# Expert gate/up with stationary weights and 88 token places, low parts made by two engines, three orders in the sparse layers

## The reference, cut to what matters

```python
def swiglu(h, wg, wu, wd):
    return (jax.nn.silu(h @ wg) * (h @ wu)) @ wd

def moe_swiglu(h, w_router, wg, wu, wd):
    logits = (h @ w_router).astype(jnp.float32)
    top_v, top_i = lax.top_k(logits, TOP_K)            # TOP_K = 2 of N_EXPERTS = 8
    w_top = jax.nn.softmax(top_v, axis=-1)
    gate = jnp.sum(jax.nn.one_hot(top_i, N_EXPERTS, dtype=jnp.float32) * w_top[..., None], axis=-2)
    out = jnp.zeros_like(h)
    for e in range(N_EXPERTS):                         # D_FF_EXPERT = 1408
        out = out + gate[..., e:e + 1].astype(h.dtype) * swiglu(h, wg[e], wu[e], wd[e])
    return out
```

## Time and profile before

| what | value |
|---|---|
| median of 3 runs | 1364.44 us (1361.74 to 1364.74) |
| the profiled execution | 1365.28 us, span 1363.5 us |
| mean granted TensorE clock | 0.993 of 2.4 GHz |
| PE busy / weight loads / DVE / ACT / POOL | 1332.1 / 1170.4 / 963.7 / 766.0 / 111.6 us |
| HBM read | 307.21 MB |

### The profile page before, as it was taken

The page is one execution under the profiler, slowest core; times in us unless marked ns, Lnnn a source line. Parts: engine busy times, 40 slices in busy tenths (PEclk is TensorE's granted clock), DMA queues, the critical chain, the costliest instruction groups (busy, mean ns, idle before and its releaser), DMA issues.

```text
span 1363.5 us, 21446 instructions
## 1 busy us (share of the span) xinstructions
PE 1332.1 (98%) x8477; PEld 1170.4 (86%) x8477; DVE 963.7 (71%) x1355; ACT 766.0 (56%) x927; POOL 111.6 (8%) x126
## 2 busy tenths in 40 slices
PE   7999999999999999999999999999999999999996
PEld 7999889888977898889999889888888888888885
DVE  6466477564867577866544465876988898998897
ACT  5565489334334348734433335753777777777674
POOL 1000031100001210000422010002000000000000
PEclk9999999999999999999999999999999999999998
DMA  7653344446534545425555536434898998999996
GB/s 284 228 191 124 139 143 152 154 159 227 202 126 152 201 176 203 171 108 186 216 186 186 186 132 228 174 126 193 318 362 332 404 361 336 394 330 365 391 421 268
DMA packets 46518, 314.72 MB, mean 231 GB/s; under 512 B 5136, under 2 KB 5392, under 8 KB 10720
## 3 DMA queue, kind: packets, MB, share of 16 engines
q1 hardware_dynamic: 42192, 297.27, 58.0%
q0 software_dynamic: 4240, 16.25, 3.4%
HBM read 307.21 MB, written 6.29 MB: 230 GB/s over the span
## 4 chain that ended last, share of the span: by engine, by line
PE 84%; DVE 7%; DMA 4%; ACT 3%; issue 1%; POOL 0%; SPq 0%; DVEq 0%; ACTq 0%
PE g_ps L647 17%; PE g_ps L649 17%; PE g_ps L648 17%; PE a_ps L647 7%; PE a_ps L649 7%; PE a_ps L648 7%; PE a_ps L652 4%; DMA raw<-w_dram 4%; DVE w_lo L1748 3%; PE a_ps L656 3%; PE o_ps L652 3%; ACT w_hi L1349 1%; DMA arena<-xT_dram 0%; PE g_ps L652 0%; PE g_ps L666 0%
## 5 line engine op out<-in xcount | busy, mean ns | idle before, releaser
L1748 DVE TENSOR_TENSOR w_lo<-raw,w_hi 128x2048 fp32r<-128x2048 f32 x218 | 502.4, 2306 | 178.2 <-ACT w_hi L1349 177.2
L1349 ACT ACTIVATE w_hi<-raw 128x2048 fp32r<-128x2048 f32 x218 | 417.4, 1914 | 251.0 <-PE a_ps L649 118.9
L647 PE MATMUL g_ps<-x_hi,w_hi 128*128 128x256 f32 x848 | 244.2, 288 | 4.7 <-ACT arena L1567 4.5
L648 PE MATMUL g_ps<-x_lo,w_hi 128*128 128x256 f32 x848 | 241.6, 285 | 0.0
L649 PE MATMUL g_ps<-x_hi,w_lo 128*128 128x256 f32 x848 | 241.4, 285 | 0.0
L647 PE MATMUL g_ps<-w_hi,x_hi 128*128 128x512 f32 (+1 forms) x584 | 217.5, 373 | 1.8 <-DVE x_lo L1841 1.0
L649 PE MATMUL g_ps<-w_hi,x_lo 128*128 128x512 f32 (+1 forms) x584 | 212.7, 364 | 0.0
L648 PE MATMUL g_ps<-w_lo,x_hi 128*128 128x512 f32 (+1 forms) x584 | 212.2, 363 | 0.0
L647 PEld LDWEIGHTS g_ps<-x_hi,w_hi 128*128 128x128 f32 x848 | 164.4, 194 | 7.6 <-issue 7.1
L649 PEld LDWEIGHTS g_ps<-x_hi,w_lo 128*128 128x128 f32 x848 | 164.4, 194 | 0.0
L648 PEld LDWEIGHTS g_ps<-x_lo,w_hi 128*128 128x128 f32 x848 | 164.3, 194 | 0.0
(11 more groups left out here) (345 smaller groups left out, 2011.6 us busy)
## 6 DMA issues: line engine op xcount, KB each, us to landing
raw<-w_dram SPq DMA_DIRECT2D x257, 1024.0 KB, 5.7
raw_in_arena<-w_dram SPq DMA_DIRECT2D x21, 1024.0 KB, 7.5
raw<-w_dram SPq DMA_DIRECT2D x4, 512.0 KB, 8.0
arena<-rows_dram POOLq DMA_DIRECT2D x2, 1024.0 KB, 6.0
table_dram<-arena POOLq DMA_DIRECT2D x2, 1024.0 KB, 9.0
arena<-table_dram POOLq DMA_DIRECT2D x2, 1024.0 KB, 13.3
arena<-xT_dram SPq DMA_DIRECT2D x2, 512.0 KB, 5.4
x<-x_dram SPq DMA_DIRECT2D x2, 512.0 KB, 7.5
```

Of the source, the lines that this page charges most:

```text
L647: pe.matmul(ps, lh, rh, start=start, stop=False, skip_group_check=True)
L648: pe.matmul(ps, lh, rl, start=False, stop=False, skip_group_check=True)
L1349: act.activation(w_hi[w_place(s)][:, :], raw[PLACE[s]][:, :], ACT.Copy).then_inc(hi_done, 1)
L1748: dve.tensor_tensor(w_lo[w_place(s)][:, :], raw[PLACE[s]][:, :], w_hi[w_place(s)][:, :].bitcast(F32), ALU.subtract).then_inc(lo_done, 1)
```

## The change

- **88 token places.** CAP = 88 replaces 128 per expert, CHUNKS = 3 rounds at most instead of 2; more than one round only if an expert has over 88 tokens. `sel`, `row_of`, `gate_of`, `back`, `o_hi`, `o_lo`, `o_rows` and `ym` shrink to 88. `x_both` holds, per block of the contraction and per expert, 88 high and 88 low columns side by side.
- **Gate/up.** The weights are the stationary side: per slot two 128-column halves (gate, up) by eight blocks, and for each a matmul of `w_hi` with 176 moving columns and one of `w_lo` with 88. The result comes out as hidden rows by tokens, so the transposes go. DVE sums the two 88-column parts (`joined`, a reduce out of PSUM), ACT applies silu in SBUF, DVE multiplies (`opened`), ACT and DVE split into `ym`. A bank of PSUM now holds one slot instead of a unit.
- **Low parts shared.** From slot MOE + 3 on DVE makes columns 0 to 1279 of `w_lo` and POOL columns 1280 to 2047 (`share`). PE and SP wait for both. POOL's row sends and table reads stand between its shares.
- **Sparse layers.** ACT's `ahead(I_KC)` stands behind the copy of the turned q. `compressed` runs between the two halves of the rows slot of step 7. The two halves of the first output slot run at steps 9 and 10.

```diff
@@ -44,6 +44,9 @@
...
 MOE = 143
+CAP = 88
+CHUNKS = -(-S // CAP)
+SHARED = 1280
 N_SLOTS = MOE + PAIRS * 33
@@ -314,15 +319,15 @@
...
-    return part[:, u % 4 // 2, (u % 2) * S:(u % 2 + 1) * S].rearrange("p (m c) -> p m c", m=2)
-def gate_of_unit(u):
-    return gate_view(u)[:, 0:S].rearrange("p (m c) -> p m c", m=2)
-def unit_half(u, which):
-    return g_ps[u % 3][:, :].rearrange("p (m g c) -> p m g c", m=2, g=2)[:, :, which, :]
+    return part[:, u % 4 // 2, (u % 2) * S:(u % 2) * S + 2 * CAP].rearrange("p (m c) -> p m c", m=2)
+def sums_of(u):
+    return gate_view(u)[:, 0:4 * CAP].rearrange("p (m g c) -> p m g c", m=2, g=2)
+def unit_bank(u, half):
+    return g_ps[(2 * u + half) % 3][:, 0:4 * CAP].rearrange("p (g a c) -> p g c a", g=2, a=2)
@@ -475,6 +481,9 @@
...
+if LAST_THERE[to] >= MOE:
+    sp.sem_inc(half_free, 1)
+    sp.wait_ge(lo_shared, LAST_THERE[to] - MOE + 1 + turn)
@@ -612,23 +621,52 @@
...
+def whole(n):
+    pool.wait_ge(lo_done, MOE + n)
+    pool.sem_inc(lo_shared, 1)
+def share(s, i):
+    slot = s + RING
+    pool.wait_ge(hi_done, slot + 1 + 33 * i)
+    pool.tensor_tensor(w_lo[w_place(slot)][:, SHARED:], raw[PLACE[slot]][:, SHARED:],
+                       w_hi[w_place(slot)][:, SHARED:].bitcast(F32), ALU.subtract).then_inc(lo_shared, 1)
+def send(e, i):
+    pool.wait_ge(m_ohi, 2 * e + 2 + 4 * i)
+    pool.sem_inc(rows_sent, 1)
+    pool.wait_ge(table_rows, 32 + 16 * e + 32 * i)
+    pool.sem_inc(rows_sent, 1)
+    pool.indirect_dma_start(o_table[:, :], bass.IndirectOffsetOnAxis(row_of[0:CAP, e:e + 1], 0),
+                            o_rows[0:CAP, e, :], None).then_inc(table_rows, 16)
+def gate_up(i, earlier):
+    for n in range(FT):
+        share(MOE + n, i)
+        if n == 2 and earlier:
+            send(1, i - 1)
+whole(1)
...
+whole(2)
+whole(3)
...
+gate_up(0, False)
...
-    for e in range(2):
-        pool.wait_ge(m_ohi, 2 * e + 2 + 4 * i)
-        pool.sem_inc(rows_sent, 1)
-        pool.wait_ge(table_rows, 32 + 16 * e + 32 * i)
-        pool.sem_inc(rows_sent, 1)
-        pool.indirect_dma_start(o_table[:, :], bass.IndirectOffsetOnAxis(row_of[:, e:e + 1], 0),
-                                o_rows[:, e, :], None).then_inc(table_rows, 16)
+    for c in range(UNITS):
+        share(MOE + FT + c, i)
+        if c == 8:
+            send(0, i)
+    gate_up(i + 1, True)
...
-pool.wait_ge(sums_in, 16)
-pool.dma_start(f_acc[:, :, :], choice_rows(1), accum_op=ALU.add).then_inc(sums_in, 16)
+for c in range(UNITS - RING):
+    share(MOE + FT + c, before)
+    if c == 4:
+        pool.wait_ge(sums_in, 16)
+        pool.dma_start(f_acc[:, :, :], choice_rows(1), accum_op=ALU.add).then_inc(sums_in, 16)
@@ -1156,16 +1196,17 @@
...
-if i == STEP_KV:
-    compressed()
...
-        rows_slot(s0 + m)
+        rows_slot(s0 + m, compressed if i == STEP_KV else None)
...
-    out_slot(L_WO[l], OUT_L, 0, (c_lo, 2 * l + 1))
+    pe.wait_ge(lo_done, L_WO[l] + 1)
+    out_mm(L_WO[l], OUT_L, 0, 0, (c_lo, 2 * l + 1))
+if i == STEP_OUT[0] + 1:
+    out_mm(L_WO[l], OUT_L, 0, 1).then_inc(used, 1)
@@ -1218,56 +1259,48 @@
...
+        mm = mm32(bank[:, :], back[0:CAP, e, t * P:(t + 1) * P], src[0:CAP, e, n * 512:(n + 1) * 512],
...
+def split_ready(s, i, whole=False):
+    pe.wait_ge(lo_done, s + 1 + 33 * i)
+    if not whole:
+        pe.wait_ge(lo_shared, s - MOE + 1 + 33 * i)
...
+    if earlier:
+        pe.wait_ge(m_xlo, 4 + 4 * i)
...
+            n = 2 * u + half
+            s, e, bank = MOE + n, n // UNITS, g_ps[n % 3]
+            if n >= 3:
+                pe.wait_ge(m_sum, n - 2 + FT * i)
+            elif earlier:
+                pe.wait_ge(m_sum, FT * i)
+            split_ready(s, i, n < RING and not earlier)
+            hi, lo = weights(s, (KD, S))
+            for which in range(2):
+                to, rows = bank[:, 2 * CAP * which:2 * CAP * (which + 1)], slice(which * P, (which + 1) * P)
...
+                    if n == 0 and which == 0 and not earlier and k % 2 == 0:
+                        pe.wait_ge(m_xlo, k // 2 + 1)
+                    pe.matmul(to, hi[:, k, rows], x_both[:, k, e, :, :].rearrange("p a c -> p (a c)"),
+                              start=k == 0, stop=False, skip_group_check=True)
+                    mm = pe.matmul(to[:, 0:CAP], lo[:, k, rows], x_both[:, k, e, 0, :],
+                                   start=False, stop=k == KD - 1, skip_group_check=True)
+            mm.then_inc(used, 1)
+        if u == TURN_SEL_AFTER:
+            if earlier:
+                pe.wait_ge(m_ohi, 4 * i)
...
+                    mm = mm32(a_ps[1][0:CAP, 2 * e:2 * e + 2], sel[:, t, e, :].bitcast(F32),
@@ -1561,10 +1592,11 @@
...
-for m in (0, I_Q[0], I_KC):
+for m in (0, I_Q[0]):
...
+ahead(s0 + I_KC)
@@ -1679,27 +1711,26 @@
...
+act.wait_ge(m_hid, u + 1 + UNITS * i)
+act.activation(ym_hi[:, 2 * u:2 * u + 2, :], hidden_of(u), ACT.Copy).then_inc(m_yhi, 1)
...
+    if u >= 1:
+        y_high(u - 1, i)
...
+    act.wait_ge(m_sum, 2 * u + 2 + FT * i)
+    act.activation(sums_of(u)[:, :, 0, :], sums_of(u)[:, :, 0, :], ACT.Silu).then_inc(m_silu, 1)
...
+    if c == 1:
+        y_high(UNITS - 1, i)
...
+        act.activation(back[0:CAP, :, :], o_ps[0:CAP, :].rearrange("p (a b) -> p a b", a=2), ACT.Copy)
@@ -1745,7 +1776,8 @@
...
-dve.tensor_tensor(w_lo[w_place(s)][:, :], raw[PLACE[s]][:, :], w_hi[w_place(s)][:, :].bitcast(F32),
+mine = slice(0, SHARED if s >= MOE + RING else SLOT)
+dve.tensor_tensor(w_lo[w_place(s)][:, mine], raw[PLACE[s]][:, mine], w_hi[w_place(s)][:, mine].bitcast(F32),
@@ -2457,37 +2491,44 @@
...
+    dve.tensor_tensor(ym_lo[:, 2 * u:2 * u + 2, :], hidden_of(u),
...
+def joined(u, half, i):
+    dve.wait_ge(used, MOE + 2 * u + half + 1 + 33 * i)
+    dve.tensor_reduce(sums_of(u)[:, half, :, :], unit_bank(u, half), AX.X, ALU.add).then_inc(m_sum, 1)
+def opened(u, i):
+    dve.wait_ge(m_silu, u + 1 + UNITS * i)
+    dve.tensor_tensor(hidden_of(u), sums_of(u)[:, :, 0, :], sums_of(u)[:, :, 1, :], ALU.mult).then_inc(m_hid, 1)
...
+            two = a_ps[1][0:CAP, 0:4].rearrange("p (a b) -> p a b", a=2)
+            dve.tensor_scalar(row_of[0:CAP, :], two[:, :, 1], const[0:CAP, C_PART:C_PART + 1], None, ALU.max)
+            dve.tensor_copy(gate_of[0:CAP, :], two[:, :, 0]).then_inc(m_back, 1)
+        joined(u, 0, i)
+        if u >= 1:
+            opened(u - 1, i)
+        ahead(s, i)
+        joined(u, 1, i)
+        if u >= 1:
+            y_low(u - 1, i)
...
+        if c == 0:
+            opened(UNITS - 1, i)
+        if c == 2:
+            y_low(UNITS - 1, i)
```

More of the change, by code:

```diff
@@ L279, in rounded @@
             return nc.alloc_sbuf_tensor_at(name, [P, *shape], F32R, offset=at)
-        sel = rounded("sel", arena_at + 4 * 6656, (NT, 2, P))
+        sel = rounded("sel", arena_at + 4 * 6656, (NT, 2, CAP))
+        x_both = rounded("x_both", x_at, (KD, 2, 2, CAP))
         back = rounded("back", arena_at + 4 * 7680, (2, S))
@@ L682, in rows_slot @@
                 for m in range(2):
+                    if m and amid:
+                        amid()
                     for k in range(KD):
@@ L1304, in down @@
                             for t in range(NT):
-                                tr = turned(o_ps[:, e * S + t * P:e * S + (t + 1) * P], sel[:, t, e, :].bitcast(F32))
+                                tr = turned(o_ps[0:CAP, e * S + t * P:e * S + (t + 1) * P], sel[:, t, e, :].bitcast(F32))
                         tr.then_inc(m_turn_sel, 1)
@@ L1721, in high_out @@
                                 act.wait_ge(used, MOE + FT + 11 + 33 * i)
[L1722 to L1723 removed]
+                            act.activation((o_hi if last else o_rows)[0:CAP, e, n * 512:(n + 1) * 512], a_ps[2 * e + n][0:CAP, :],
+                                           ACT.Copy, scale=gate_of[0:CAP, e:e + 1]).then_inc(m_ohi, 1)
                     gate_up(0)
@@ L2009, in gate_weights @@
                 on1, on2 = t3(32), t3(48)
-                own(dve.tensor_scalar(ranks[:, 0, :, NE:2 * NE], gate, -1.0 - P, None, ALU.add))
+                for half in range(1, CHUNKS):
+                    own(dve.tensor_scalar(ranks[:, 0, :, half * NE:(half + 1) * NE], gate, -1.0 - CAP * half, None, ALU.add))
                 for t in range(NT):
-                    for half in range(2):
+                    for half in range(CHUNKS):
                         own(dve.tensor_scalar(ranks[:, 2, t, half * NE:(half + 1) * NE], on2[:, t, :],
@@ L2466, in gate_up @@
                         s = MOE + 2 * u
-                        ahead(s, i)
                         if u == TURN_SEL_AFTER + 1:
@@ L2588, in expert_slots @@
         two = gu[:, :, 2 * u:2 * u + 2].transpose(1, 0, 2, 3, 4)
-        halves = [two[:, :, m] for m in range(2)] if u == 5 else [two[:, 4 * h:4 * h + 4] for h in range(2)]
-        up += [h.reshape(1, P, SLOT) for h in halves]
+        up += [two[:, :, m].reshape(1, P, SLOT) for m in range(2)]
     return np.concatenate(up + [wd.reshape(FT // 2, 2, P, D).transpose(0, 2, 1, 3).reshape(FT // 2, P, SLOT)])
```

110 lines of the change are left out of this document (24 added, 86 removed).

## The result

The changed kernel takes 1482.5 us (median of 4 runs, 1476.25 to 1487.87) against 1363.1 for the kernel before beside it: ratio 1.088 (95% interval 1.082 to 1.093), 119 us slower. The forecast was 1440, range 1410 to 1485, 0.94 on slower. The direction held, and the time lies inside the range, 43 us above the forecast. The weight loads and the turn-taking are there, but the turns don't set the pace of gate/up, and the 43 us are a term that stood at nothing, TensorE's clock.

A forecast was written before the change was run, and what follows sets the result against it. PE was taken as the bound, its time being columns streamed. Gate/up +65, down +9 and +4, hand-overs +4 gave +82; orders -6: 1365.3 + 82 - 6 = 1441, against the median 1440; range 1410 to 1485.

The forecast's parts named there:

- Loads, 0.111 us each, slot 3.55: Gate/up on PE: 32 weight loads per slot at 0.111 us make 3.55 us, against 2.76 before; +15.0 us per pair.
- rival (a): Expert stage: turns hide, only weight loads count, +60, down unchanged, orders -6: 1419 us; chance 0.18.
- Turn-taking: Expert stage: DVE and POOL alternate on low parts, 1.46 + 1.82 = 3.28 us per slot, where it was 2.29.
- Gate/up runs at about 3.61 whatever the loads turn out to cost: Gate/up: DVE and POOL turns take 3.61 us per slot against PE's 3.55; +16.3 us per pair, +65 for four.
- Pairs 116 to 120 us apart: Expert stage: listed as a sign of being right, the distance from one pair of experts to the next.
- the +3 of turns in down: Down: low parts 3.28 us per slot against PE's 2.76, plus token selection; +3.0 per pair, +9; last pair +4.
- Table read-back: Last down: the read-back moved there must arrive before slot eleven, at 34 us; fits barely, otherwise up to 5 us.
- Orders, -6: Sparse layers: three reorderings remove PE waits of 2.48, 0.48 and 0.79 us per layer; 3 to 9 us gained, 6 taken.
- The extra rank rows are a few small DVE operations once, under 1 us: DVE work for the additional rank rows: done once, counted among what costs nothing, under 1 us.
- The clock at nothing in the sum: Expert stage: the sum held no term for a lower TensorE clock; a falling clock appeared only as a rival.
- rival (d): Expert stage: the clock falls to half pace, slot 7.1 us, +340 if it lasts, about 1700 us; chance 0.03.
- a granted clock of 0.5 in the stage: Expert stage: listed among the signs that would show the forecast wrong.

The follow-up runs named there:

- the stretch put back: The changed kernel with all low parts made by VectorE, plus PE holding the first pair's eleventh slot until DVE summed the tenth: 1478.3 us, 1.086.
- the burst: The changed kernel plus 16 unneeded 512-column matmuls on PE ahead of the sixth unit of the first pair's gate/up: 1452.6 us, 1.065.

## Why the prediction was right or wrong

- **Loads, 0.111 us each, slot 3.55: right.** 0.112 and 3.57; alone they cost 65 us where rival (a) had 60. The Trainium skill ("TensorE: Matmul & The Clock Gate", "LDWEIGHTS (loading the stationary operand)") has columns over 1.2 GHz, 107 ns; at full clock the trace agrees within 5 ns, at the low one it shows 213, which that rule doesn't tell.
- **Turn-taking: right.** 1.49 alone, 3.14 for POOL behind DVE, PSUM sums untouched. The trace bears out the Trainium skill's "SBUF — State Buffer", "Who interferes with whom", an exclusive pair of ports for these two engines.
- **"Gate/up runs at about 3.61 whatever the loads turn out to cost": wrong.** The turns leave DVE 0.18 us idle per slot, and 542 matmuls in 60 us stand in the shared kernel as in the one without sharing. The two limits lay 0.06 us apart per slot, so this hardly touched the sum.
- **Pairs 116 to 120 us apart: the number was right** where the clock stayed up (`row_of` at 1162.7, 1281.4, 1398.7: 118.7 and 117.3), the reason wasn't. Loads alone give 113.4. The 5.3 and 3.9 us over it are PE's loop, 2.66 and 2.32 us, and about half of the time at 0.50 behind each, 5.4 and 3.1 us with PE at work. Nothing is left for the +3 of turns in down, and PE isn't idle behind `w_lo` there. The last down has 0.60 and 0.32 us of it, where +4 stood. The turns come out when the loop doesn't hold PE, as 4 us of waiting for the selection.
- **Table read-back "fits, or up to 5 us": near the upper end.** DVE waited 2.56 us for the table, PE 1.23 for DVE's `o_lo` behind that, and the chain of waits of the changed kernel ends through POOL's queue:

```profile
1458.61 2.55 POOL w_lo L631
1461.16 12.00 DMA y_spare<-rows_dram
```

  The last norm's rows are asked for behind the read-back and the last low parts, 9 us ahead of the end of the last scatter where it was 34, and land 2.6 us after it. From the last scatter to the end it is 15.5 us where it was 11.6.
- **Orders, -6: wrong, 0.** I priced the waits that went and not the ones next in line, DVE and ACT a few us later.
- **"The extra rank rows are a few small DVE operations once, under 1 us": wrong, and where the idle stretch began.** The added operations themselves cost 0.5 us (2.2 to 2.7 with all low parts on DVE); the 3.2 us up to 5.9 are POOL's turns, behind which the whole of `gate_weights` stood. I priced them without the turn that I had priced for everything else. It isn't the one cause: spread over five units it left a stretch as well.
- **The clock at nothing in the sum, and 0.03 on rival (d): the step that failed.** (d) was priced for the whole stage and came true for one pair. The first gate/up took 122.1 us, the others 79.2, and 4 us of down behind it ran at 0.50 too: 43 + 2 = 45 us in this execution. I had held against (d) that a whole pair ran at 1.00; that pair streamed 512 columns and had no idle stretch, and says nothing on a thin stream with one. (Its price was off too: a slot of 7.1 us gives 4 x (22 x 7.1 - 63.1) = +372, not +340.)

The account, with the kernel before on each chip taken off: 1363 + 65 (loads, tail) + 12 (PE's loop and the turns) + 43 (clock) = 1483, with 0 for the orders. As differences along a chain of runs these must add up; that the 43 is the clock rests on the 45 above, on the stretch put back (+41 to +44) and on the burst (30 back). Without the clock the sum is +77 against the forecast's +76, though 60 + 22 - 6 stood there for 65 + 12 + 0: that these agree is luck. Luck too is that the range held the time: its upper part was drawn for turns, and what filled it was the clock, which by the prediction's own list, "a granted clock of 0.5 in the stage", was a sign of being wrong.

## What to carry to other kernels

Before a stream of wide matmuls is traded for one that is bound by weight loads, ask what happens when it is interrupted once: the same stream then went on at 1.2 GHz for 88 us, and 88 columns more per pair of matmuls, which cost nothing under the loads, or 5.5 us of wide ones, brought 44 and 30 us back. Work given to GpSimd beside VectorE must be priced on VectorE's smallest operations too, and on what waits for them. A wait removed is worth what the next one leaves of it.

## What the runs showed of the hardware that I had not expected

- The interval between weight loads follows the granted clock: 0.112 us at 1.00, 0.213 at 0.50.
- An idle stretch of 0.86 us in the thin stream (264 columns per two loads) was followed by clock 0.50 until the wide matmuls; one of 0.89 us in a stream of 352 columns per two loads was not. The same way, the loop stretches of 2.66 and 2.32 us behind the thin stream were followed by 6.8 and 3.4 us at 0.50, and those of 2.77 and 2.56 behind the wider one by none.
- PE stands 2.0 to 4.7 us at the start of its loop's second and third round in the changed kernels, labelled as a wait for DVE or as issue, and doesn't when the loop is written out. That it is the fetching of instructions was only argued; the kernel before has the same loop and no such stretch.
